# Rotation by a lane shuffle on VectorE, and a last down projection in two halves of its columns

## The reference, cut to what matters

```python
xr = x.reshape(B, L, N_HEADS, 2, 2, 2, HEAD_DIM // 4)
x0, x1 = xr[..., 0, :], xr[..., 1, :]
out = jnp.stack([x0 * c - x1 * s, x0 * s + x1 * c], axis=-2)
```

## Time and profile before

| | us |
|---|---|
| median of 3 runs | 1998.23 |
| lowest and highest run | 1997.45, 1999.3 |
| the profiled execution | 2003.98 |
| its span, first to last instruction | 2002.2 |

### The profile page before, as it was taken

The page is one execution under the profiler, slowest core; times in us unless marked ns, Lnnn a source line. Parts: engine busy times, 40 slices in busy tenths (PEclk is TensorE's granted clock), DMA queues, the critical chain, the costliest instruction groups (busy, mean ns, idle before and its releaser), DMA issues.

```text
span 2002.2 us, 29614 instructions
## 1 busy us (share of the span) xinstructions
PE 1789.3 (89%) x12220; PEld 1378.4 (69%) x12220; DVE 841.4 (42%) x1696; ACT 310.8 (16%) x707; POOL 111.1 (6%) x120
## 2 busy tenths in 40 slices
PE   7999999999999999989999999999999865665766
PEld 2788888888884779669999998878778321121212
DVE  3766666964431156644675237533433000000001
ACT  2200000011210111422111124212322000000000
POOL 2000000010100010000000002602001000000000
PEclk9999999999999999999999999989999887777777
DMA  8343444965442115116545863000459899999995
GB/s 360 122 137 127 134 137 155 357 212 190 149 146 84 63 43 169 42 64 232 188 168 169 294 209 126 24 22 24 147 223 385 356 430 433 431 433 429 432 431 232
DMA packets 46612, 426.15 MB, mean 213 GB/s; under 512 B 5315, under 2 KB 5796, under 8 KB 15532
## 3 DMA queue, kind: packets, MB, share of 16 engines
q1 hardware_dynamic: 36864, 387.04, 50.3%
q10 hardware_dynamic: 9644, 37.59, 5.3%
HBM read 423.56 MB, written 1.05 MB: 212 GB/s over the span
## 4 chain that ended last, share of the span: by engine, by line
PE 30%; DMA 19%; DVE 3%; POOL 1%; issue 1%; ACT 1%; SPq 0%; DVEq 0%; POOLq 0%; ACTq 0%
DMA arena<-experts_ring_dram 19%; PE bank L961 14%; PE bank L1136 6%; PE bank L1527 3%; PE bank L1799 2%; PE bank L1359 1%; DVE arena L2944 0%; PE bank L1630 0%; PE bank L1678 0%; PE bank L1409 0%; POOL rstd L872 0%; DVE rstd L2327 0%; PE bank L1849 0%; PE bank L1721 0%; POOL arena L936 0%
## 5 line engine op out<-in xcount | busy, mean ns | idle before, releaser
L961 PE MATMUL bank<-arena 128*128 128x256 f32 (+2 forms) x3296 | 626.6, 351 | 6.7 <-DVE arena L2795 2.0
L961 PEld LDWEIGHTS bank<-arena 128*128 128x128 f32 x3296 | 532.4, 192 | 91.4 <-issue 33.3
L1799 PE MATMUL bank<-arena 128*32 128x512 f32 x1528 | 246.6, 803 | 152.8 <-DMA arena<-experts_ring_dram 151.9
L1799 PEld LDWEIGHTS bank<-arena 128*32 128x32 f32 x1528 | 66.1, 141 | 325.0 <-issue 321.3
L1085 PE MATMUL bank<-arena 128*128 128x256 f32 x880 | 193.9, 379 | 0.0
L1085 PEld LDWEIGHTS bank<-arena 128*128 128x128 f32 x880 | 167.1, 190 | 23.1 <-issue 0.5
L1136 PE MATMUL bank<-arena 128*128 128x128 f32 x1512 | 169.2, 275 | 0.0
L1136 PEld LDWEIGHTS bank<-arena 128*128 128x128 f32 x1512 | 169.1, 192 | 0.1
L3135 DVE TENSOR_TENSOR arena<-arena,bank 128x512 f32<-128x512 f32 x8 | 5.5, 688 | 229.9 <-PE bank L1799 229.9
L2491 DVE SCALAR_TENSOR_TENSOR arena<-arena 128x1024 f32<-128x1024 f32 x56 | 68.3, 1220 | 0.0
L3141 DVE COPY arena<-bank 128x512 f32<-128x512 f32 x4 | 2.8, 690 | 145.8 <-PE bank L1799 145.8
(11 more groups left out here) (414 smaller groups left out, 1905.8 us busy)
## 6 DMA issues: line engine op xcount, KB each, us to landing
arena<-dense_dram SPq DMA_DIRECT2D x167, 1024.0 KB, 4.9
arena<-experts_ring_dram SPq DMA_DIRECT2D x41, 4096.0 KB, 26.9
arena<-ada_rest_dram ACTq DMA_DIRECT2D x56, 512.0 KB, 5.6
arena<-experts_dram SPq DMA_DIRECT2D x19, 1024.0 KB, 9.6
arena<-ada_head_dram SPq DMA_DIRECT2D x8, 1024.0 KB, 24.0
arena<-experts_dram SPq DMA_DIRECT2D x8, 512.0 KB, 9.9
arena<-experts_ring_dram SPq DMA_DIRECT2D x2, 2048.0 KB, 24.5
arena<-tokens_dram ACTq DMA_DIRECT2D x1, 2048.0 KB, 21.2
```

What stands on the lines that cost most here:

```text
L961: ins = mm(out, lhsT=w, rhs=rhs(k), start=k == 0, stop=k == k_tiles - 1)
L1799: ins = mm(ps[banks[half]][32 * e:32 * e + 32, :], lhsT=lhs[:, 2 * kp + par, CAP * e:CAP * e + CAP], rhs=slab[e][par][:, half * 512:half * ...
```

## The change

- The rotation no longer uses TensorE. VectorE shuffles the lanes of `raw_v` (halves of 16 within each group of 32 partitions change places), multiplies by the cosines, then multiplies the shuffled tile by sines that carry the sign in the constant `rope`, and adds. A semaphore `turned` counts finished tiles; ScalarE's copy of tile n waits for tile n - 2. `perm` leaves the constants `small` (64 KB). Banks 5 and 6 are not used in this stage for rotations.
- The 16 transposes of `u` are issued four at a time behind the products of tiles 8, 9, 10 and 11, and each of the copies to `utok` stands behind VectorE's work for that tile.
- In the last group the down projection runs first for columns 0 to 511 over the whole contraction, then for 512 to 1023; the last four ring steps are laid out for that on the host. Between the two stand the scatter of the first half and statistics 0 to 3; behind the second the scatter of the second half and statistics 4 to 7. The last step arrives as 2, 1 and 1 MB. VectorE copies the second half out only after its first two additions to `x`. The other groups keep their products; their scatter waits for bank 1 only ahead of its second half.

```diff
             for n in range(16):
...
                 product(ps[n % 4][:, 0:w_n], KD, lambda k: h1[:, k, 0:w_n], full[n % 4])
-                if n:
-                    rotate(n - 1)
-            rotate(15)
-
-            pe.wait_ge(hyena_ready, 8)
-            for n in range(4):
-                kt, half = n // 2, n % 2
-                take(pe, "ut", 5 + half, n // 2)
-                for q_ in range(4):
-                    ins = nc.tensor.transpose(ps[5 + half][:, q_ * P:q_ * P + P],
-                                              u[:, half * 4 + q_, kt * P:kt * P + P], ident)
-                ins.then_inc(full[5 + half], 1)
+                if n == 8:
+                    pe.wait_ge(hyena_ready, 8)
+                if 8 <= n < 12:
+                    gated_to_tokens(n - 8)
...
+            def last_down(half):
+                take(pe, "moe", half, (N_GROUPS - 1) * 2 + 1)
+                for kp in range(KD // 2):
+                    turn, j = divmod(EX_STEPS - 4 + 2 * half + kp // 2, 4)
+                    if kp % 2 == 0:
+                        pe.wait_ge(ex_step_in[j], 16 * (turn + 1))
+                    for par in range(2):
+                        if half and kp == KD // 2 - 1:
+                            pe.wait_ge(ex_last_in[par], 16)
+                        for e in range(GROUP):
+                            o = ((kp % 2 * 2 + par) * GROUP + e) * (D // 2)
+                            ins = mm(ps[half][32 * e:32 * e + 32, :], lhsT=hidT[:, 2 * kp + par, CAP * e:CAP * e + CAP],
+                                     rhs=ex_step[j][:, o:o + D // 2], start=kp == par == 0, stop=kp == KD // 2 - 1 and par == 1)
+                            if kp % 2 == par == e == 0:
+                                ins.then_inc(ex_started, GROUP)
+                ins.then_inc(full[half], 1)
...
+                if last:
+                    for half in range(2):
+                        evacuated(pe, "moe", 5 + half, i * 3)
+                    last_down(0)
+                    scatter(0)
+                    for j in range(4):
+                        stat(15, j, T)
+                    last_down(1)
+                    scatter(1)
+                    for j in range(4, KD):
+                        stat(15, j, T)
+                    return
...
-                    evacuated(act, "qk", 5 + n % 2, n // 2 - 1)
+                    act.wait_ge(turned, n - 1)
...
-                got(dve, "qk", b, n // 2)
+                evacuated(dve, "qk", n % 4, n // 4)
                 if n >= 2:
 
-                    evacuated(dve, "qk", b, n // 2 - 1)
+                    dve.wait_ge(turned, n - 1)
                 r = rt[:, (n % 2) * T:(n % 2) * T + T]
-                do(tt_(r, ps[b][:, 0:T], rope[:, 1, :], mult))
+                do(V.stream_shuffle(r, raw_v[:, n % 2, :], halves_swapped))
                 do(tt_(dst, raw_v[:, n % 2, :], rope[:, 0, :], mult))
                 settle()
-                tt_(dst, dst, r, add).then_inc(evac[b], 1)
+                do(tt_(r, r, rope[:, 1, :], mult))
+                settle()
+                tt_(dst, dst, r, add).then_inc(turned, 1)
```

More of the change, by code:

```diff
@@ L187, in constants @@
     ang = (rc * invf[p % 16][:, None]).astype(f32)
-    out["rope"] = np.concatenate([np.cos(ang), np.sin(ang)], axis=1).astype(f32)
+    turn = np.where(p % 32 < 16, -1.0, 1.0).astype(f32)[:, None]
+    out["rope"] = np.concatenate([np.cos(ang), turn * np.sin(ang)], axis=1).astype(f32)
     eye = np.eye(P, dtype=f32)
     blk = (p[:, None] // 64 == p[None, :] // 64).astype(f32)
[L191 to L196, removed]
     nobwd0 = np.ones((P, 1), f32)
@@ L210, in constants @@
     iota = np.broadcast_to(np.arange(1, CAP + 1, dtype=f32), (P, CAP))
-    out["small"] = np.concatenate([eye, np.ones((P, P), f32), blk, perm, nobwd0, headsel.reshape(P, 64), iota, adasel], axis=1)
+    out["small"] = np.concatenate([eye, np.ones((P, P), f32), blk, nobwd0, headsel.reshape(P, 64), iota, adasel], axis=1)
     out["headbc"] = headbc.reshape(HEADS, HEADS * P)
@@ L570, in build @@
         ex_step_in = [sem(f"ex_step_in{i}") for i in range(4)]
-        ex_last_in = sem("ex_last_in")
+        ex_last_in = [sem(f"ex_last_in{i}") for i in range(2)]
         ex_started = sem("ex_started")
@@ L639, in build @@
         mix_ready = sem("mix_ready")
+        turned = sem("turned")
         gate_done = sem("gate_done")
@@ L843, in _ @@
             sp.wait_ge(ex_started, GROUP * (EX_STEPS + 3))
-            for par in range(2):
-                o = slice(par * GROUP * D, par * GROUP * D + GROUP * D)
+            for n, (lo, hi) in enumerate(((0, 2), (2, 3), (3, 4))):
+                o = slice(lo * SLAB, hi * SLAB)
                 sp.dma_start(ex_step[1][:, o], dram["experts_ring"][EX_STEPS - 1][:, o])\
-                    .then_inc(ex_last_in if par else ex_step_in[1], 16)
+                    .then_inc(ex_last_in[n - 1] if n else ex_step_in[1], 16)
             for q_ in range(4):
@@ L1202, in _, with gated_to_tokens @@
             tiles("z", 24, KD, lambda k: h1[:, k, 0:T], T, norm=1, after=ctx_norms)
[L1204 to L1209, removed]
+            def gated_to_tokens(n):
+                kt, half = n // 2, n % 2
+                take(pe, "ut", 5 + half, n // 2)
+                for q_ in range(4):
+                    ins = nc.tensor.transpose(ps[5 + half][:, q_ * P:q_ * P + P],
+                                              u[:, half * 4 + q_, kt * P:kt * P + P], ident)
+                ins.then_inc(full[5 + half], 1)
             for n in range(16):
@@ L1284, in hyena_out @@
                 return ins
[L1286 to L1287 removed]
+            pe.wait_ge(turned, 16)
             for b in range(4):
@@ L1785, in step_slabs, with group_product @@
                 pe.wait_ge(ex_step_in[j], i * 48 + 16 * (turn + 1))
[L1786 to L1788 removed]
                 return [[ex_step[j][:, (2 * e + par) * D:(2 * e + par) * D + D] for par in range(2)]
                         for e in range(GROUP)]
[L1792 to L1793 removed]
+            def last_down(half):
[14 more added lines that the diff above has]
+                ins.then_inc(full[half], 1)
+            def group_product(banks, kp, lhs, i, step):
+                slab = step_slabs(i, step)
                 for par in range(2):
[L1795 to L1796 removed]
                     for half in range(2):
@@ L1832, in group, with scatter @@
                     ins.then_inc(full[5 + half], 1)
+                def scatter(half):
+                    evacuated(pe, "moe", half, i * 2 + 1)
+                    evacuated(pe, "moe", 7, i)
+                    for n in (2 * half, 2 * half + 1):
+                        b, k = scatter_fills(i, last)[n]
+                        take(pe, "moe", b, k)
+                        for q_ in range(2):
+                            dt = 2 * n + q_
+                            ins = mm(ps[b][:, q_ * T:q_ * T + T], lhsT=ys4[:, dt * P:dt * P + P],
+                                     rhs=OHT, start=True, stop=True)
+                        ins.then_inc(full[b], 1)
+                if last:
[10 more added lines that the diff above has]
+                    return
                 take(pe, "moe", 0, i * 2 + 1)
@@ L1837, in group @@
                         evacuated(pe, "moe", 5 + kp // 2, i * 3)
[L1838 to L1851, removed]
+                    group_product((0, 1), kp, hidT, i, 8 + kp)
+                gather("moe", i * 3 + 1, i + 1)
+                scatter(0)
+                scatter(1)
             def gate_start(i):
@@ L3146, in group @@
                 for n, (b, k) in enumerate(scatter_fills(i, last)):
+                    if last and n == 2:
+                        second_half_out()
                     got(dve, "moe", b, k)
```

35 lines of the change are left out of this document (18 added, 17 removed).

## The result

| | median, us | runs |
|---|---|---|
| before | 1998.76 | 1996.89 to 2000.87 |
| changed | 1989.65 | 1984.19 to 1994.36 |

The ratio is 0.9946, with a 95% interval of 0.993 to 0.9963: 10.8 us faster (7.4 to 14.0) on 1998.23. The forecast was 15.1 us, 1983.1. Direction right, size too large by 3 to 4 us; the median lies 0.15 us above the stated range, the time by the ratio (1987.4) within it.

A forecast was written before the change was run, and what follows sets the result against it. TensorE bounds the query and key stage, DMA 1555 to 1980 us, then an uncovered chain to the end. Gains of 9.0 + 0.1 + 1.2 + 4.8 = 15.1 us give 1983.1 us, range 1979.5 to 1989.5.

The forecast's parts named there:

- Part 1: Query and key stage: without rotations on TensorE the value products start 9.0 us earlier (8.6 and 9.25 as other values).
- Shuffle: VectorE in the query and key stage: a lane shuffle of 128x256 takes 0.42 us and is hidden, costing 0.
- cover ends when the shuffle needs over about 2 us: Query and key stage: past about 2 us a shuffle, VectorE's work per tile is no longer hidden behind TensorE.
- Rival 4: Query and key stage: transposes between products lower the clock, two insertions give back 13.7 us, 1997 us; chance 0.03.
- Carried to the end one to one: From the query stage through the DMA-bound expert stage: transfers start earlier by what TensorE wins, so the whole gain survives.
- rival 2: Expert stage: expert weights bound its start, so the query stage's gain is not carried; 6.1 us gained, 1992; chance 0.05.
- Part 2: Last down projection by column halves: last weights land as before, the end after them shortens by 3.2 to 8.0 us.
- (a): First half of the last projection: its scatter and statistics 0 to 3 make TensorE start the next step 2.4 us late.
- (b): Second half of the last projection: the lateness is made up and VectorE's copy starts 1.2 us earlier.
- about 7 us of slack: Last projection: argument against a late second half, that the 9.7 us between steps leave this slack, used only once.
- rival 1: Last projection: the second half comes late at half clock, copy 1 to 3 us later; 11 us gained, 1987; chance 0.15.
- (c): End, VectorE's copy to the last root: only half the scatter and statistics remain, 4.8 us won, between 4.2 and 6.0.

The follow-up runs named there:

- e8: The whole change with each tile's shuffle issued eight times, against the kernel before; median 1986.07 us, ratio 0.9932.
- e7: The kernel before, unchanged, profiled again to see how far its own profile moves; one run, 2000.76 us.
- e10: The whole change with statistics 0 to 3 moved behind the scatter of the second half, against the kernel before; median 1990.37 us, ratio 0.9953.
- e9: The kernel before with each rotation product issued four times, against the kernel before; median 2017.3 us, ratio 1.0086.
- e6: The kernel before with five filler products ahead of the attention norm's wait for VectorE's reciprocal, against the kernel before; median 1999.24 us, ratio 0.9996.

## Why the prediction was right, and where its size was off

- *Part 1 in its stage*: 9.0 forecast, 9.25 measured, the upper of its three values; the transposes cost 0.44 a group, not 0.49.
- *Shuffle*: 0.42 forecast, 0.434 measured; hidden. The estimate that the forecast worked out from the Trainium skill, "VectorE: DVE Perf Modes" (The perf-mode tier table), 0.3 us plus overhead, agrees with 0.13 us of overhead. But "cover ends when the shuffle needs over about 2 us" was wrong: e8 spent eight shuffles a tile and lost 0.26 us. Comparing the work of one tile with the pitch of one tile left out that four banks and two raw places let VectorE lag, and that the wide tiles let it catch up.
- *Rival 4, clock under the transposes*: absent; 1.00 over the stage, against what the forecast cited from the Trainium skill, "TensorE: Matmul & The Clock Gate" (Part 4: PE-mode transpose). The runs show this for groups of 4 to 8 transposes among matmuls; a long run of transposes alone is not in them.
- *"Carried to the end one to one"*: D is 425.1 to 425.7 in all fourteen profiles, whatever came before, and C does not grow with the new rotation, so the expert stage starts and ends with TensorE's progress and rival 2 is out. The step that failed is the assumption that nothing on the way gives anything back: B is 223.0 to 224.1 in every profile with the new rotation and no filler, against 220.2 to 220.6 in three of four with the old, some 3 us. It was the clock after a 2.3 us wait, and filling the wait took it away. That it is the position of the wait in time that decides was not tested by itself; and e7 shows the long form without the change.
- *Part 2 (a), (b)*: forecast late by 2.4 us and full again in time. Late it was, by 2.3 (e10's second half starts with its data 9.73 us ahead of the last weights, the changed kernel's 7.43), and the copy came 1.14 us behind the last weights, at most 1.77, where 2.98 stood before: 1.8 us won, forecast 1.2. The "about 7 us of slack" of rival 1 was too much: at full clock a step takes 3.64 (e10) of 9.7 us, and the earlier trace rows show waits of 3.1 to 4.6.
- *Part 2 (c)*: 11.07 to 5.53 us, 5.5 won, forecast 4.8. This number is in part luck. Of the 5.5, 3.65 are the change's at equal clock and 1.9 the clock's; the forecast's upper end, 6.0, compared the lower clock before with the full clock after. Together E fell from 14.05 to 6.67, by 7.4. Over all profiles it fell by less: the old end is 14.05 three times and 12.6 and 12.4 once each (mean 13.4), the new one 6.67 four times and 7.9 and 8.9 once each (mean 7.3), 6.2 between the means.
- *Sum*: 9.25 + 7.4 - 3 = 13.6 by the profiles, or 9.25 + 6.2 - 2.0 = 13.4 by the means of E and B, where both measurements of the whole give 10.8 (up to 14.0) and 12.2 (up to 15.4). The last 1 to 3 us were not located and may be noise; e9's 17.2 for 20.0 points the same way. Against one profile each this would have been hidden: 18.0 us. The absolute forecast also took over from one execution that the profiled one lies 5.75 us above the median; the changed one lay 3.7 below.
- *Rival 1's number*: its 11 us and 1987 match the ratio's 10.8 and 1987.4, but not by its mechanism. It had the copy 1 to 3 us later against the last weights, and the copy came earlier in every profile with this end. That the median lies 0.15 us from the edge of the range is luck as well: its runs spread over 10 us.

## What to carry to other kernels

Time taken from the engine that bounds a stage can reach the end through a later DMA-bound stage if the transfers there are released by that engine, as here (D within 0.6 us whatever was saved ahead of it); check that by the releases, not by the DMA's share. Work that hangs on the last transfer is what to cut: split the output rather than the contraction, so that evacuation, scatter and statistics of the first half go under the transfers. A smaller last transfer helped in the profile, not visibly in the times. And a forecast for a kernel like this one, whose TensorE waits 1 to 3 us in a few places, should carry several us for the clock, compare stretches at equal clock, and read more than one profile before it credits a stretch.

## What the runs showed of the hardware that I had not expected

- A wait of 2.33 us with the same work on both sides led to 4.28 us or 7.01 us for the same 16 rows of matmuls, at a mean granted clock of 0.76 (over 14 us) or 0.62 (over 17 us).
- Two executions of the kernel before differ by 4.7 us at the first raw copy, 4.0 in B and 2.5 in C. Over all fourteen profiles the unchanged C runs from 666.1 to 674.4, in the order of its granted clock (0.97 to 0.85 over 100 us of it), while the stretch that weights bound repeats within 0.6 us in 425.
- The same code from copy to root took 9.18 us at a mean clock of 0.98 (e6) and 11.07 at 0.79.
- A lane shuffle of 128x256 float32 costs 434 ns, as much as a multiplication of that size (425), and its selector load 14 ns.
